# The channel norm's gains move into the gather ring, three first weight groups are issued ahead of their regions, and the mixing matrices are built where z lay

## What is computed

```
h = x + mixer(rmsnorm(x, g_mix))            # 8 retention heads and 4 mLSTM heads, w_in (2048 x 7176), w_out
c = rmsnorm(h, g_ffn)                       # the channel norm
idx, gate = top 16 of 256 pairs, for 8 heads, of c @ w_peer_q against two key tables   # 128 experts a token
h = h + sum_k gate_k * gelu(c . u[idx_k]) * v[idx_k]      # u, v: 16384 x 2048 each
h = h + sigmoid(rmsnorm(h, g_ple) @ w_ple_gate) * (p @ w_ple_proj)
y = rmsnorm(h, g_final)
```

## Time and profile before

| | before |
| --- | --- |
| three runs | 3990.47 (median), 3985.92, 4010.08 us |
| profiled execution | 4015.72 us; its span 4013.9 us |
| PE, DVE, ACT, POOL busy | 79%, 69%, 17%, 37% |
| DMA | 1474 MB, mean 367 GB/s over the span |

### The profile page before, as it was taken

One profiled execution on the slowest core, in us unless ns is written; L12 is line 12 of the kernel. 1 busy time (PEld: TensorE's weight loads), 2 busy tenths in 40 slices (PEclk: granted clock), 3 DMA queues, 4 the chain that ended last, 5 costly groups with the idle time before them and its releaser, 6 DMA issues.

```text
span 4013.9 us, 27355 instructions
## 1 busy us (share of the span) xinstructions
PE 3170.2 (79%) x9486; PEld 1691.8 (42%) x9486; DVE 2751.7 (69%) x3851; ACT 674.3 (17%) x1639; POOL 1470.4 (37%) x900
## 2 busy tenths in 40 slices
PE   8997788998891158999878506589999999996867
PEld 4546333553481024445436505434444444442323
DVE  1007966677689676886646988868888887776561
ACT  1212110222020112112302208600000000002011
POOL 0002544545433533454334342333444333334530
PEclk9998799999995588999989756589999999998988
DMA  7889999999996989999999879999999999999856
GB/s 261 279 280 359 415 373 382 411 402 414 376 399 249 415 330 379 390 409 393 340 342 411 342 300 326 345 414 421 419 413 421 421 421 413 421 416 402 351 216 220
DMA packets 365745, 1474.03 MB, mean 367 GB/s; under 512 B 27688, under 2 KB 66024, under 8 KB 231016
## 3 DMA queue, kind: packets, MB, share of 16 engines
q0 software_dynamic: 129024, 939.58, 58.2%
q1 hardware_dynamic: 225216, 515.54, 34.5%
q10 hardware_dynamic: 11368, 17.17, 1.2%
HBM read 1446.50 MB, written 25.69 MB: 367 GB/s over the span
## 4 chain that ended last, share of the span: by engine, by line
PE 39%; DMA 30%; DVE 14%; issue 12%; ACT 3%; POOL 1%; SPq 1%; ACTq 0%; another core or an unknown queue 0%; DVEq 0%; POOLq 0%
PE psum L704 24%; PE psum L1013 10%; DMA W<-in_w_in 7%; DMA actT<-a_scratch 7%; DVE ring L1992 6%; DMA ring<-in_peer_v,eidx 3%; DMA ring<-in_peer_u,eidx 3%; DMA W<-in_w_out 3%; DMA a_scratch<-W 2%; DVE arena L2004 2%; DMA W<-in_w_ple_gate 2%; DMA W<-in_w_peer_q 1%; POOL ring L668 1%; ACT W L1389 1%; PE psum L1066 1%
## 5 line engine op out<-in xcount | busy, mean ns | idle before, releaser
L668 POOL DMA_INDIRECT ring<-in_peer_u,eidx x576 | 888.6, 1543 | 1555.8 <-DVE dots L1992 1110.2
L1992 DVE CUSTOM_DVE_ANT_0 ring<-ring,cx 128x2048 f32<-128x2048 f32 x576 | 1308.6, 2283 | 105.5 <-DMA ring<-in_peer_u,eidx 103.5
L704 PE MATMUL psum<-W,actT 128*128 128x512 f32 x2752 | 1246.9, 611 | 118.5 <-DMA W<-in_w_in 65.4
L668 POOL DMA_INDIRECT ring<-in_peer_v,eidx x320 | 581.6, 1818 | 852.1 <-DVE arena L2004 799.9
L704 PEld LDWEIGHTS psum<-W,actT 128*128 128x128 f32 x2752 | 534.0, 196 | 787.6 <-issue 678.3
L2004 DVE SCALAR_TENSOR_TENSOR arena<-ring,wts,arena 128x2048 f32<-128x2048 f32 x320 | 751.2, 2347 | 51.7 <-DMA ring<-in_peer_v,eidx 43.9
L1013 PE MATMUL psum<-arena 128*128 128x512 f32 x1024 | 446.9, 597 | 18.1 <-DMA arena<-in_peer_v 14.9
L1013 PE MATMUL psum<-W,arena 128*128 128x512 f32 x1024 | 456.4, 607 | 0.0
L704 PE MATMUL psum<-W,arena 128*128 128x512 f32 x768 | 350.8, 613 | 53.2 <-DMA W<-in_w_out 52.2
L1013 PEld LDWEIGHTS psum<-W,arena 128*128 128x128 f32 x1024 | 200.2, 197 | 246.5 <-issue 246.2
L1013 PEld LDWEIGHTS psum<-arena 128*128 128x128 f32 x1024 | 194.9, 192 | 258.8 <-issue 254.8
(11 more groups left out here) (246 smaller groups left out, 1965.6 us busy)
## 6 DMA issues: line engine op xcount, KB each, us to landing
W<-in_w_in SPq DMA_DIRECT2D x168, 1024.0 KB
arena<-in_peer_v SPq DMA_DIRECT2D x64, 1024.0 KB
W<-in_peer_v SPq DMA_DIRECT2D x64, 1024.0 KB
W<-in_w_out SPq DMA_DIRECT2D x48, 1024.0 KB
W<-in_w_peer_q SPq DMA_DIRECT2D x48, 1024.0 KB
W<-in_w_ple_gate SPq DMA_DIRECT2D x48, 1024.0 KB
a_scratch<-W SPq DMA_DIRECT2D x64, 256.0 KB
actT<-a_scratch SPq DMA_DIRECT2D x32, 512.0 KB, 26.4
```

Source lines behind the costliest of these rows:

```text
L668: pool.indirect_dma_start(ring[:, slot, :], None, a["peer_u" if what == "u" else "peer_v"][0], off(ix, 0)).then_inc(ring_in[slot], 16)
L704: ins = pe.matmul(bank(4 * s + j), lhs(k, j), W[:, k, :], start=(k == 0), stop=(k == KT - 1))
L1992: dve.tensor_tensor_reduce(row, row, cx[:, :], 1.0, 0.0, ALU.mult, ALU.add, dots[:, n % DEEP, c:c + 1]).then_inc(u_used, 1)
```

## The change

1. g_ffn is no longer loaded by ACT into `cx`. It becomes a member "c" of POOL's gather order and takes a slot of the ring; DVE reads it there and writes `cx`. The slots are now dealt in turn within three parts of the order (rows to 143, to 383, and the rest), "c" among the `u`.
2. SP loads the first group of `w_ple_gate` for block 0 and for blocks 1 to 3, and the first group of `w_in` for mixer 2, before it waits for the region `X`. Mixer 2's x loads wait for the last projection (`e_proj`) and, for block 4's, for `y_ready`, no longer for the y store (`y_out`); ACT waits for that store before it writes z.
3. The build's buffers move from `W` to `X`, so that the even `v_tiles` lie in `W`, and the first four are loaded as soon as mixer 2's last weight has been used. The wait for block 3's picks moves from SP to DVE, ahead of the build.
4. Numbers of the order: `EMBED_AT` 0 at 141.4 (141) and 1 at 547 (548), `PICK_STEP` 2 at 10 (9), `DENSE_AT` at 416.5 (417).

```diff
-EMBED_AT = {0: (141, 1.6), 1: (548, 1.15), 2: (700, 1.0)}
-PICK_STEP = {1: 4.0, 2: 9.0}
+EMBED_AT = {0: (141.4, 1.6), 1: (547, 1.15), 2: (700, 1.0)}
+PICK_STEP = {1: 4.0, 2: 10.0}
...
-DENSE_AT = (417, 4.0)
+DENSE_AT = (416.5, 4.0)
...
+        if what == "w":
+            continue
+        at = ROW0[x] if what == "c" else x
+        if at < ALONE[0]:
+            part, slots = "first", (0, 1, 2, 3) if what != "v" else (4, 5, 6, 7)
+        elif at < ALONE[1]:
+            part, slots = "alone", (0, 1, 2, 3, 4, 5)
+        else:
+            part, slots = "last", (0, 1, 2) if what != "v" else (3, 4, 5)
+        slot = slots[turn[part, slots] % len(slots)]
...
-        first_u, second_u = (Wf[:, x:x + TOKENS].bitcast(U32) for x in (0, TOKENS))
+        first_u, second_u = (X[:, x:x + TOKENS].bitcast(U32) for x in (0, TOKENS))
...
-            return (X[:, 0:VT * D] if m % 2 == 0 else Wf).rearrange("p (x d) -> p x d", x=VT)
+            return (Wf if m % 2 == 0 else X[:, 0:VT * D]).rearrange("p (x d) -> p x d", x=VT)
...
             if g == 2:
-                sp.wait_ge(picked[1], PAIRS)
-                sp.wait_ge(moved, 1)
-                sp.wait_ge(y_out, 16)
+                load_w(sp, a["w_in"][0], "in", g, range(0, 1))
+                sp.wait_ge(e_proj, DG)
             for j, t in enumerate(grp):
+                if t == SB:
+                    sp.wait_ge(y_ready, 1)
                 load_x(sp, t, xa(g, j), x_in[j])
...
+            if e == 1:
+                sp.wait_ge(d_done, 4 * (NVG - 1))
+            if e < 2:
+                load_w(sp, a["w_ple_gate"][0], "ple", e, range(0, 1))
             if e == 0:
                 sp.wait_ge(picked[1], PAIRS)
...
         def sp_dense(sp):
+            sp.wait_ge(mm, prod.end("q", 2))
+            load_tiles(sp, 0)
...
-            sp.wait_ge(picked[3], PAIRS)
-            sp.wait_ge(moved, 2)
...
+                if what == "c":
+                    pool.dma_start(ring[:, slot, :], a["g_ffn"][0:1, :].to_broadcast([P, D])).then_inc(ring_in[slot], 16)
...
+                    if g == 2 and i == 0 and j == 0:
+                        act.wait_ge(y_out, 16)
...
-                if u + 1 == ROW0[t] + ROWS[t] and t + 1 < NB:
-                    load_gain(act)
...
             yield build_at(-2)
-            dve.wait_ge(mm, prod.end("q", 2))
+            dve.wait_ge(moved, 2)
+            dve.wait_ge(picked[3], PAIRS)
...
-                    dve.wait_ge(g_in, 16 * (x + 1))
+                    slot, arrival, _ = plan[what, x]
+                    dve.wait_ge(ring_in[slot], 16 * arrival)
                     dve.wait_ge(n_rs, i + 1)
-                    dve.scalar_tensor_tensor(out=cx[:, :], in0=hslot(x), scalar=ncol(i, 3), in1=cx[:, :],
+                    if x:
+                        dve.wait_ge(u_used, ROW0[x])
+                    dve.scalar_tensor_tensor(out=cx[:, :], in0=hslot(x), scalar=ncol(i, 3), in1=ring[:, slot, :],
```

More of the change, by code:

```diff
@@ L214, in ring_plan @@
 def ring_plan():
[L216 removed]
+    plan, last, arrivals, turn = {}, {}, Counter(), Counter()
     for what, x in gather_order():
[L218 to L227 removed]
+        if what == "w":
[8 more added lines that the diff above has]
+        slot = slots[turn[part, slots] % len(slots)]
+        turn[part, slots] += 1
+        arrivals[slot] += 1
+        plan[what, x] = (slot, arrivals[slot], last.get(slot))
+        last[slot] = (what, x)
     return plan
@@ L576, in residual @@
                         load_x(sp, t, hslot(t), hx_in[j])
-            load_w(sp, a["w_in"][0], "in", g)
-            load_w(sp, a["w_out"][0], "out", g, residual)
+            load_w(sp, a["w_in"][0], "in", g, range(1 if g == 2 else 0, ZG))
+            load_w(sp, a["w_out"][0], "out", g, None, residual)
             load_w(sp, a["w_peer_q"][0], "q", g)
@@ L623, in sp_dense @@
                     sp.wait_ge(d_done, 4 * (m - 1))
[L624 to L626 removed]
+                if m:
+                    load_tiles(sp, m)
         def load_final(sp, e):
```

67 lines of the change are left out of this document (29 added, 38 removed).

## The result

| | before | after |
| --- | --- | --- |
| median of 20 runs each | 4009.27 us (3985.92 to 4026.08) | 3982.05 us (3962.77 to 4025.32) |
| ratio, 95% interval | | 0.9928 [0.9913, 0.9943] |
| profiled execution | 4015.72 us, span 4013.9 | 3966.93 us, span 3965.1 |

The change makes the kernel faster by 0.72%, 29 us (23 to 35). The forecast was 3950 us, as 40.5 us off a median of 3990.5. That median was of three runs; with 20 it is 4009.3. Of the 32 us between the forecast and the measured time, 19 come from that base and 13 from the sum (27 us between the two medians, 29 by the ratio). The run of 4025.32 us is a slow one, which the ratio leaves out. One profile of each shows -48.8 us, more than the medians; the part "Open" further down says what is known of that.

A forecast was written before the change was run, and what follows sets the result against it. No engine was taken as the bound (PE busy 79%); DMA transfers set the pace in mixer 2 and the dense product. Terms -2.5 - 12 - 13 + 1 - 10 - 4 = -40.5 us off 3990.5 gave 3950 us, range 3908 to 4000.

The forecast's parts named there:

- first gate group of block 0: Load moved into the DMA hole before 1350: -10.5 us by bytes, -33 by PE's waits; -12 taken.
- mixer 2's start: x issued sooner, w_in landing before x_sample: 16 us on PE's side, 10.5 by bytes; -13 (-8 to -17).
- gains in the ring, block 2: Boundary 1 to 2: DVE's 20.84 us wait goes, most returns as waits for rows or weights; -3 (+5 to -15).
- block 3: Boundary 2 to 3: the gain's slot, free only after row 383, undoes the prefetch; +1.5 instead of -7.6 us.
- block 1: Boundary 0 to 1: no gain wait to remove, and POOL, on the path, issues one more load; +2.5 us.
- tiles ahead: Dense product: first tiles land in the hole after mixer 2's last weight, 4.19 MB fewer in a DMA-bound stage; -10 (to -15).
- first gate group of blocks 1 to 3: Last stage: PE starts sooner without its gate wait, -8, against +4 for standing a row earlier; -4 (-10 to +6).
- rival by which PE's waits count in full: Whole kernel: row gathers have slack, so every removed PE wait counts; about -78, 3912 us; chance 0.15.
- the loads are taken back: Rival: gathers take the moved loads' place; only the kernel's start and dense bytes stay, -2.5 - 10, 3978 us; chance 0.2.
- two signs of being wrong: PE's mixer 2 waits for w_in grow by its start's gain, or DVE's for in_peer_u grow at rows 128-135, 512-520.
- third rival: Block boundaries: each of four gains holds POOL and drains the ring, 12 us each, 49 in all; 4027 us; chance 0.13.
- The rule of the Trainium skill: POOL's loads are slowed by DVE's two-port mode, SP's and ACT's not: five gains cost 13.7 instead of 1.8 us of issue.

The follow-up runs named there:

- loads0_only: Kernel before, with only block 0's first gate group and mixer 2's first w_in group moved ahead and x not waiting for the y store; ratio to before 0.9927.
- win_back: Changed kernel with mixer 2's first w_in group loaded behind the x loads again; ratio to before 0.9939.
- gate1_back: Changed kernel with the first gate group of blocks 1 to 3 loaded behind p and w_ple_proj again; ratio to before 0.9908.
- c_split: Changed kernel with the mLSTM state C's store and load split into four pieces by head, n's store behind them; ratio to before 0.9901.
- best1: Changed kernel with the gate group of blocks 1 to 3 behind p again and the ring's last u slots dealt 1, 2, 0; ratio to before 0.9913.

## Why the prediction was right and where it was wrong

| term | forecast | in the traces |
| --- | --- | --- |
| start | -2.5 | -1.7 |
| first gate group of block 0 | -12 | -13.4 (B) |
| mixer 2's start | -13 | -9.5 (C) |
| gains in the ring, block 2 | -3 | -3.3 (D +1.5, E -4.8) |
| block 3 | +1.5 | -0.6 (F) |
| block 1 | +2.5 | +6.6 (A) |
| tiles ahead | -10 | -11.9 (G) |
| first gate group of blocks 1 to 3 | -4 | +13 (H) |
| sum | -40.5 | -20.8, ratio -29 |

**Right.** The gate group of block 0, which lands in a hole before a full stretch, gave back about its bytes (10.5 us) and not PE's wait: 13.4 us of 33. The tiles fit the same rule, 12 us, with the reserve above. The rival by which PE's waits count in full would have had B fall by 33 us, and it is out. The loads were not taken back either: loads0_only keeps its 29 us to the end. That the measured 3982 us lie beside the 3978 of this rival ("the loads are taken back") is owed to the base and is no point for it: by gains, 29 us stand between its 12.5 and the forecast's 40.5. The range of 3908 to 4000 holds the measured time, the forecast's own of 3930 to 3968 does not, and the largest chance (0.48) had gone to a change within 1%, which this is. Of the two signs of being wrong that it named, PE's waits for `W<-in_w_in` in mixer 2 did not grow (18.3 us before, 12.9 after), but DVE's for `in_peer_u` behind block 1's start did (5.1 to 10.5 us in its first 16 rows), at block 4's they did not.

**Right in size, wrong in its reason: block 2, -3.** The 20.84 us came back within 16 rows, as DVE's waits for PE and ACT and not for rows or weights, as the prediction had it. It took mixer 2 to be bound by transfers; in this stretch PE was busy without a pause at the full clock, before and after, so up to row 272 the wait was not on the path.

**Right: block 3.** At block 3 the slot undid the prefetch as worked out: a wait of 5.86 us and F as long as before, and with the other turn of slots the wait was gone.

**The step that failed: "first gate group of blocks 1 to 3", -4 (-10 to +6).** It measured +13. The prediction counted what PE would no longer wait for, the gate, and asked nothing of what the four quarters would stand before. p, needed first, is issued on the same queue behind them: PE's wait for it grew from 13.70 to 34.22 us, more than the 10.98 us that went. The term is wrong by 17 us, more than the 11.5 us by which the sum exceeds the measured gain. The +4 for the number 547 was not seen either. It is also the part of the change that the experiments say to undo.

**The same omission in "mixer 2's start", -13.** I wrote that w_in lands before x_sample rather than beside it. It did, and x_prompt waited for it: PE's start gained 6.7 us, not 16. Here it cost little, since win_back, without that delay, has the same C (184.4 and 185.6 us). With it goes the other half of the term, the bytes of the moved group (10.5 us): C gives no sign of them. The 9.5 us measured go with x's earlier issue.

**Mis-sized: block 1, +2.5.** The issue of the gain cost 0.60 us, not 0.94 to 2.74. What costs is the slot: a row's gather waits for the product that frees it (4.18 us), at a boundary where the prediction had POOL on the path. DVE's waits for gathered `u` rows in A grew from 5.1 to 10.5 us, which is most of the 6.6; that they go back to this one wait was not tried. It is the drained ring of the third rival, at one boundary and for 7 us, not at four for 12.

**The rule of the Trainium skill** (DMA: Bandwidth & Descriptors, SWDGE vs HWDGE vs iDMA), by which the prediction gave all five gains POOL's longer time of 2.74 us, did not show: the five issues took 0.57 to 0.71 us each, three of them with DVE idle and two beside its additions (0.60 and 0.58), while the gathers took 0.93 to 3.05. The page speaks of DVE's two-port mode, and no view here tells in which mode those additions ran, so this is no case against the rule; what failed is the step from a gather's time to that of a plain copy.

**Open.** The profile of after is 48.8 us below that of before, the medians 29: after's E is one of the two short ones, worth 20 us against the other five, and its G (1192.4) is the shortest of all, 12 us below the mean of its eleven. The sum of the traces' terms, -20.8, is 8 us short of the ratio's 29; no stretch that I cut holds the rest.

## What to carry to other kernels

A load moved ahead on a queue delays what is issued behind it while it is under way (p: 5.6 us to land in front of the gate, 30.8 behind it): before moving it, list those and ask which the waiting engine needs first. A prefetch into a hole was worth about its bytes at most (13.4 us of a 33 us wait at block 0, nothing that could be told for w_in), not the wait that it removes. A wait of one engine costs nothing while another, on which the next steps hang, works without a pause: look at that one before pricing the wait. And once waits are removed, an engine comes sooner to the next load it needs: look for the one that then lands too late (here 512 KB of state). To see parts of 5 to 15 us in a kernel whose executions scatter by 40, cut all traces at the same instructions and compare groups.

## What the runs showed of the hardware that was not expected

A direct copy of 1 MB issued by POOL costs it 0.57 to 0.71 us, less than any gather (0.93 us at best); only two of the five stood beside work of DVE. A 512 KB transfer in rows of 1 KB took 18.7 us to land, and the load behind it 24.3, in a stretch where the DMA was full (gate1_back); in four pieces of 128 KB (c_split), stores took 7.5 us each and loads 6.5, in the median. In win_back PE waited 3.30 us for C, and the granted clock was 1.00 before it, 0.63 in the 4 us behind it and 0.50 in the 6 us behind those, with PE busy 3.94 and 6.00 us of them (the first 128x256 pair took 0.67 us, the next 1.20, at the 1.2 GHz level). In best1 it waited 1.11 us, and the clock stayed at 1.00.
